# One chunk of expert weights per round, loaded as four transfers instead of one

## What is computed

```python
logits = jnp.dot(t, w_router, preferred_element_type=f32) + b_router
top_v, top_i = lax.top_k(logits, TOP_K)          # TOP_K = 4 of N_EXPERTS = 32
gates = jax.nn.softmax(top_v, axis=-1)
...
def expert_block(args):                          # xb: the tokens of expert e
    xb, e = args
    hid = xb @ w_e1[e] + b_e1[e]                 # w_e1: (32, 1024, 2048)
    gate = jnp.minimum(hid[:, :D_FF], SWIGLU_LIMIT)
    lin = jnp.clip(hid[:, D_FF:], -SWIGLU_LIMIT, SWIGLU_LIMIT)
    act = gate * jax.nn.sigmoid(SWIGLU_ALPHA * gate) * (lin + 1.0)
    return act @ w_e2[e] + b_e2[e]               # w_e2: (32, 1024, 1024)
```

## Time and profile before

| | |
|---|---|
| median of 3 runs | 1276.53 us |
| lowest and highest | 1276.32 and 1279.07 us |
| the profiled execution, its time | 1282.41 us |
| its span (first to last instruction) | 1280.3 us |
| mean granted clock of PE | 0.992 |
| PE busy | 1246.3 us (97%) |
| DVE, ACT, POOL busy | 410.8, 170.9, 113.3 us |
| DMA over the span | 455.97 MB, mean 356 GB/s |

### The profile page before, as it was taken

How to read it: one execution, slowest core, us unless ns; L and a number is a source line. 1 busy time by engine, 2 the same in 40 slices (tenths; PEclk the granted TensorE clock), 3 DMA queues, 4 the chain that set the end, 5 groups by cost and what they waited for, 6 DMA issues and landing times.

```text
span 1280.3 us, 15124 instructions
## 1 busy us (share of the span) xinstructions
PE 1246.3 (97%) x6111; PEld 561.9 (44%) x6111; DVE 410.8 (32%) x845; ACT 170.9 (13%) x299; POOL 113.3 (9%) x107
## 2 busy tenths in 40 slices
PE   8999999999999999999999999999999999999997
PEld 4488886759543333333333333333333333333332
DVE  6789685376432111211121111121111112111111
ACT  2043333011211000000100000000000000000002
POOL 4599400010000000000000000000000000000000
PEclk9999999999989999999999999999989999999999
DMA  8743476582889999999999999999999999999995
GB/s 255 174 165 132 103 149 229 204 305 82 343 312 430 425 427 426 428 427 427 429 426 428 428 426 429 429 427 429 429 425 429 427 427 430 427 427 430 428 426 244
DMA packets 56036, 455.97 MB, mean 356 GB/s; under 512 B 4888, under 2 KB 7136, under 8 KB 31024
## 3 DMA queue, kind: packets, MB, share of 16 engines
q1 hardware_dynamic: 53168, 450.80, 85.8%
q0 software_dynamic: 1664, 3.90, 2.2%
q10 hardware_dynamic: 1152, 0.52, 0.3%
HBM read 453.07 MB, written 1.61 MB: 355 GB/s over the span
## 4 chain that ended last, share of the span: by engine, by line
PE 82%; DMA 14%; ACT 2%; DVE 1%; issue 1%; SPq 0%; DVEq 0%
PE pt L1158 27%; PE pt L1181 16%; PE pt L619 10%; DMA ring<-in_w_e 10%; PE pt L646 6%; PE pt L1083 4%; PE pt L606 4%; PE pt L584 4%; PE pt L1067 3%; DMA low<-in_w_e 3%; PE pt L656 2%; PE pt L1148 2%; ACT wi_ L1328 1%; DMA stage<-in_w_in 1%; PE pt L1033 0%
## 5 line engine op out<-in xcount | busy, mean ns | idle before, releaser
L1158 PE MATMUL pt<-ring,uT_ 128*64 128x512 f32 x1192 | 266.3, 595 | 3.9 <-DMA ring<-in_w_e 3.9
L1158 PEld LDWEIGHTS pt<-ring,uT_ 128*64 128x64 f32 x1192 | 83.2, 137 | 179.1 <-issue 170.1
L2089 DVE COPY ct_<-ct_ 128x2 f32 x31 | 5.3, 170 | 452.7 <-PE pt L1158 445.3
L1181 PE MATMUL pt<-ring,wi_ 128*64 128x512 f32 x560 | 124.5, 595 | 3.7 <-ACT wi_ L1328 3.7
L1158 PE MATMUL pt<-stage,uT_ 128*64 128x512 f32 x400 | 92.6, 610 | 5.1 <-issue 3.6
L1158 PE MATMUL pt<-low,uT_ 128*64 128x512 f32 x384 | 86.3, 595 | 1.5 <-DMA low<-in_w_e 1.5
L619 PE MATMUL pt<-spare,stage 128*128 128x256 f32 x384 | 84.2, 380 | 0.0
L1511 ACT ACTIVATE wi_<-pt 128x512 f32<-128x512 f32 x32 | 19.1, 598 | 454.4 <-PE pt L1158 454.4
L2173 DVE TENSOR_SCALAR wi_<-pt 128x512 f32<-128x512 f32 x32 | 22.1, 692 | 177.7 <-PE pt L1158 177.7
L619 PEld LDWEIGHTS pt<-spare,stage 128*128 128x128 f32 x384 | 72.5, 190 | 10.6 <-issue 0.7
L1181 PEld LDWEIGHTS pt<-ring,wi_ 128*64 128x64 f32 x560 | 38.9, 137 | 77.0 <-issue 72.0
(11 more groups left out here) (354 smaller groups left out, 1267.9 us busy)
## 6 DMA issues: line engine op xcount, KB each, us to landing
ring<-in_w_e SPq DMA_DIRECT2D x112, 2048.0 KB, 27.1
low<-in_w_e SPq DMA_DIRECT2D x38, 2048.0 KB, 26.2
stage<-in_w_e SPq DMA_DIRECT2D x36, 2048.0 KB, 28.0
stage<-in_w_in SPq DMA_DIRECT2D x16, 1024.0 KB, 7.2
stage<-in_w_xkv SPq DMA_DIRECT2D x8, 1024.0 KB, 5.3
ring<-in_w_mix_out SPq DMA_DIRECT2D x4, 1024.0 KB, 9.2
stage<-in_w_xq SPq DMA_DIRECT2D x4, 1024.0 KB, 17.1
ring<-in_w_xo SPq DMA_DIRECT2D x4, 1024.0 KB, 6.8
```

The source lines that it names most:

```text
L1158: last = pe.matmul(pt[u][SLOTS * g:SLOTS * (g + 1), 512 * b:512 * (b + 1)], x[:, k % 4, k // 4], w, start=(k == 0), stop=(k == KD - 1))
L1181: last = pe.matmul(pt[u][SLOTS * h:SLOTS * (h + 1), at:at + 512], hidden[:, c, g], ring_slot[n][:, D * c + 512 * h:D * c + 512 * (h + 1)], ...
```

## The change

In rounds 1 to 5 the round's first chunk (expert 5, 10, 15, 20 or 25, chunk 0 of `w_e1`) is no longer loaded by one transfer of 128 rows but by four:

- rows 0 to 111 in full (112 rows of 16 KiB), which counts on the slot's semaphore as before;
- rows 112 to 127, columns 0 to 1023 (16 rows of 4 KiB);
- rows 112 to 119, columns 1024 to 4095 (8 rows of 12 KiB);
- rows 120 to 127, the same columns (8 rows of 12 KiB).

The last three count on `s_lead`, 48 for each round. PE waits for `s_lead` at `q * 48 + 48` as well as for the slot, ahead of that chunk. Five chunks of the 192 are touched; the bytes and their places are the same.

```diff
--- before.py
+++ after.py
@@ -40,6 +40,7 @@
 CHUNK = 4096
 HALF = CHUNK // 2
 RING = 10
+WHOLE_ROWS, SHIFTED_COLS, EIGHT = 112, 1024, 8
 W1_CHUNKS, W2_CHUNKS = 4, 2
 CHUNKS = W1_CHUNKS + W2_CHUNKS
 ROUND = 5
@@ -174,7 +175,7 @@
         s_con = sem("identity_loaded"); s_tables = sem("const_tables_loaded"); s_x = [sem(f"x_tile{t}_loaded") for t in range(NT)]; s_gain = sem("gains_loaded"); s_small = sem("s5_small_loaded")
         s_bc = sem("b_and_c_loaded"); s_par = sem("small_parameters_loaded"); s_mem = sem("mem_loaded")
         s_u4 = sem("u4_regrouped"); s_tapw = sem("taps_written"); s_tap0 = sem("lag0_taps_written"); s_toep = sem("toeplitz_loaded")
-        s_rt = sem("router_and_biases_loaded"); s_gf = sem("lower_bias_and_final_gain_loaded"); s_lead = sem("first_half_chunks_loaded")
+        s_rt = sem("router_and_biases_loaded"); s_gf = sem("lower_bias_and_final_gain_loaded"); s_lead = sem("first_half_chunks_and_shifted_rows_loaded")
         s_out = sem("out_written")
         s_slot = [sem(f"slot{i}_loaded") for i in range(STAGE)]
         s_used = sem("slots_used")
@@ -307,6 +308,15 @@
             dram, c = (w1_dram, j) if j < W1_CHUNKS else (w2_dram, j - W1_CHUNKS)
             src = dram[e, c] if isinstance(e, int) else dram[bass.ds(e, 1), c].rearrange("a p n -> p (a n)")
             eng.dma_start(ring_slot[n], src).then_inc(s_chunk[n], 16)
+
+        def load_shifted(eng, e, n):
+
+            src = w1_dram[bass.ds(e, 1), 0].rearrange("a p n -> p (a n)")
+            dst = ring_slot[n]
+            eng.dma_start(dst[0:WHOLE_ROWS], src[0:WHOLE_ROWS]).then_inc(s_chunk[n], 16)
+            eng.dma_start(dst[WHOLE_ROWS:P, 0:SHIFTED_COLS], src[WHOLE_ROWS:P, 0:SHIFTED_COLS]).then_inc(s_lead, 16)
+            for row in range(WHOLE_ROWS, P, EIGHT):
+                eng.dma_start(dst[row:row + EIGHT, SHIFTED_COLS:], src[row:row + EIGHT, SHIFTED_COLS:]).then_inc(s_lead, 16)
 
         block = ctx.enter_context(nc.Block())
 
@@ -406,16 +416,19 @@
             sp.wait_ge(S["prod"], MX + 7)
             load_page(sp, "w_xo", R21)
 
-            def load_block(e, q, r, first=0):
-
-                for j in range(first, CHUNKS):
+            def load_block(e, q, r, shifted=False):
+
+                for j in range(CHUNKS):
                     opening = isinstance(q, int) and q == 0
                     back, was = freed_by(opening, r, j)
                     if was < W1_CHUNKS:
                         sp.wait_ge(m_w1u, W1_CHUNKS * (q * ROUND + back) + was + 1)
                     else:
                         sp.wait_ge(m_w2u, W2_CHUNKS * (q * ROUND + back) + was - W1_CHUNKS + 1)
-                    load_chunk(sp, e, place_at(opening, r, j)[0], j)
+                    if shifted and j == 0:
+                        load_shifted(sp, e, place_at(opening, r, j)[0])
+                    else:
+                        load_chunk(sp, e, place_at(opening, r, j)[0], j)
 
             sp.wait_ge(S["prod"], XQ + 8)
             load_chunk(sp, 1, 8, 3)
@@ -444,7 +457,7 @@
                 load_block(r, 0, r)
             with sp.Fori(1, ROUNDS) as q:
                 for r in range(ROUND):
-                    load_block(q * ROUND + r, q, r)
+                    load_block(q * ROUND + r, q, r, shifted=(r == 0))
             for i, (b, j) in enumerate(LAST):
                 back, was = divmod(i - RING, CHUNKS)
                 if was < W1_CHUNKS:
@@ -1184,7 +1197,7 @@
                 if cs[-1] == 3:
                     last.then_inc(m_w2u, 1)
 
-            def block_of(it, q, r, early=None):
+            def block_of(it, q, r, early=None, extra=False):
 
                 pe.wait_ge(m_xT, 1 if early == 0 else it + 2)
                 for j in range(W1_CHUNKS):
@@ -1192,6 +1205,8 @@
                     pe.wait_ge(s_chunk[n], loaded)
                     if early == 0 and j == 0:
                         pe.wait_ge(s_lead, 48)
+                    elif r == 0 and j == 0 and not extra:
+                        pe.wait_ge(s_lead, q * 48 + 48)
                     if early == 0 and j == 1:
                         pe.wait_ge(m_xT, 2)
                     if j == 1:
@@ -1303,7 +1318,7 @@
                 with pe.Fori(0, EXTRA // ROUND) as g:
                     for i in range(ROUND):
                         with pe.If(n_extra > g * ROUND + i):
-                            block_of(g * ROUND + NE + i, g + (NE + i) // ROUND, (NE + i) % ROUND)
+                            block_of(g * ROUND + NE + i, g + (NE + i) // ROUND, (NE + i) % ROUND, extra=True)
             with pe.If(n_extra < 1):
                 last_blocks()
             pe.wait_ge(m_y, NE + n_extra)
```

## The result

| | before | with the change |
|---|---|---|
| median | 1278.24 us (6 runs) | 1328.62 us (6 runs) |
| lowest and highest | 1276.32 to 1279.40 us | 1322.02 to 1337.42 us |
| profiled execution, its time | 1282.41 us | 1331.54 us |
| its span | 1280.3 us | 1329.6 us |

The ratio is 1.0404, with a 95% interval of 1.0379 to 1.0429: slower by some 50 us. The forecast was 1298 us with a range of 1274 to 1316 us. The direction was right, and the size was not: 50 us instead of 22.

A forecast was written before the change was run, and what follows sets the result against it. Gapless DMA transfers were taken as the bound. Terms 4.29 + 0.59 + 4.43 = 9.31 us against 4.90 cost 4.4 us a round, 22 us in five, giving 1298 us from 1276.5, range 1274 to 1316 us.

The forecast's parts named there:

- What bounds the kernel: Expert loop: gapless DMA transfers at 428 GB/s and share 1.01 set the pace, then an untouched tail of 21.6 us.
- The ring's reserve: Rival in the expert loop: chunks already held in the ring hide the loss; given almost no chance.
- Issues and PE's wait: SP's queue and PE at a round's head: three more issues, one more wait, priced at nothing; uncovered issues 5.5 us.
- The 112 rows: Large piece of the cut chunk: runs at the full rate like 128 rows, 4.29 us a round.
- The other end: Upper bound for the 112-row piece: half the rate, 8.6 us, 4.3 us more a round.
- The 112 rows collide too: Rival: seven rows per engine break the 128-row pattern and halve the rate, 21 us more, around 1320 us; chance 0.13.
- The pieces of eight rows: Two 98.3 KB pieces of the cut chunk: 55 GB/s, 3.55 us for both, 4.43 us with another writer joining.
- a fifth writer: During the eight-row pieces, next-chunk traffic joins four writers, each getting a fifth instead of a fourth: 3.55 to 4.43 us.
- the 16 rows: The 65.5 KB piece of 4 KiB rows: 111 GB/s, 0.59 us a round, against 0.15 us at full rate.
- The main doubt of the forecast: POOL's 16-partition Toeplitz loads: their 111 GB/s might come from 512-byte pieces instead of few partitions.
- Evening out: Rival: eight-row pieces load the leading engines, so the last finishes 2.3 us sooner, 1274.2 us; chance 0.20.
- The signs: Expected in the trace: loop at about 415 GB/s, PE chunk waits before 1080 us, DMA waits about 9 + 22 us.

The follow-up runs named there:

- The twenty added transfers of eight rows: Changed kernel with whole chunks plus four unused eight-row 4 KiB transfers a round: 1289.67 us (ratio 1.0109) on neighbouring rows, 1290.30 us (1.0099) on rows four apart.
- the engines in step: Changed kernel plus SP waiting before each round until the previous chunk landed: 1320.75 us; the same wait with whole chunks: 1297.43 us.
- round 5 alone: Changed kernel with the four-transfer load only in the last of the five rounds, whole chunks in the others: 1289.84 us, ratio 1.0085.

## Why the prediction was wrong

**What bounds the kernel: right.** Nearly all of the 49 us is lost in the transfers of the loop, at an unchanged share of 1.01; nothing gives it back; the tail is still 21.7 us long. The ring's reserve hid none of it.

**Issues and PE's wait at nothing: right.** The four transfers by columns have them all, at a ratio of 0.9997.

**The 112 rows: the step that failed.** The prediction took the full rate, 4.29 us, since "112 rows lie much nearer to 128". Measured are 7.67 us each of five in a row, and 8.24 us alone. The other end that it kept, half the rate or 8.6 us, is where they are. The row that it was held nearest to was the wrong one: 128 rows are a case of their own, and 112 behave like 64. The rival "The 112 rows collide too" had this: the rate nearly halves, and with 7.67 us the term is 5 x 3.4 = 17 us more. It was given 0.13, and had neither the cheaper small pieces nor the growth, so that its 1320 us is near the measured time in part by luck. Its reason, that the engines no longer fill the partitions in the pattern of 128 rows, isn't shown by any run. The transfer needs no neighbour to be slow.

**The pieces of eight rows: mis-sized the other way.** 55 GB/s and a fifth writer made 4.43 us of two pieces. Eight neighbouring rows alone move at 91 GB/s, 1.1 us for 98.3 KB, so 2.2 us for both. In the first dip of the changed kernel their sixteen packets take 1.11 us each on the mean, and two on each of eight engines are again 2.2 us. With 0.5 us for the 16 rows (130 GB/s alone; there 0.31 us a packet) the small pieces are 2.7 us, not 5.0, which is 5 x 2.3 = 12 us less. The twenty added transfers of eight rows don't settle it: scaled to the bytes of the pieces they are 4.2 us a round by their times and 2.8 by the trace. The main doubt of the forecast, that 111 GB/s came from pieces of 512 bytes, was not what went wrong: 16 rows of 16 KiB run at 100 to 130 GB/s. The 54 GB/s for eight rows that the prediction worked out from the Trainium skill, page "SBUF — State Buffer", section "Door 1: The DMA port swizzle", don't agree with the measured 91 either.

**Sum by measured prices.** 7.7 + 0.5 + 2.2 = 10.4 us against 4.9, so 5.5 us a round. The first dip lost 5.4 us, and with the engines in step it is 4.6 us on the mean. Five times 5.5 are 27 us, close to the 22 of the forecast, because its two errors, +17 and -12 us, nearly cancel.

**The growth: missing.** The remaining 20 us (47.2 - 27) are that a late round costs more than the first, up to 12.9 us. The prediction had the engines out of step ("5.1 us behind at the end") and used it only as a gain. The runs show it the other way: the further they are out of step, the longer the packets of whole chunks on some engines run beside the cut chunk on others, and those packets are slow as well (at least 43 in round 1, 260 in round 5). Holding the engines in step took both away, and round 5 alone costs what its own spread says. Why a whole chunk's packets slow down beside the cut isn't shown. In numbers the loss of the change is 4.8 us + 0.8 x the spread to within 1 us, a fit and no more; for two halves of 64 rows it grows half as fast, from 6.7 us at a spread of 2.2 to 8.8 us at 7.4.

**Evening out: never seen.** It needed few rows at no extra cost. The dips are there in every kernel with a cut by rows, and the spread at the last dip has grown from 6.5 to 10.1 us.

**The signs.** 415 GB/s was right for the first stretch (416), too high for the others. PE's waits began before 1080 us, at 786, as forecast, and came to 49.5 us instead of 31. As a sign of collisions it named that "the 112-row transfer itself lands late". The group of those five transfers ends with

```profile
DMA to landing us min/median/max: 17.6/49.2/57.6
```

against a median of 25.2 us. Alone this would prove little, since a whole chunk into `ring` takes 34.6 us from 600 to 800 us, too, where it took 21.0: in a slower stream everything lands late. The transfers by themselves decided it.

No version beats the kernel before. Cut by columns it is the same, and every cut by rows among the kernels run is slower. Whether the engines could be evened out with transfers of every second row was not tried; the spread of 6.5 us, shared between both halves of the engines, is worth 3.3 us at most by an estimate from that spread.

## What to carry to other kernels

Cut a large load by columns and keep all 128 partitions: four pieces cost nothing here, while a cut by rows, even at 112, ran the piece at 60% of the rate and slowed the whole chunks beside it. When a stream is bound by transfers at full share, price each new shape by itself, five in a row behind the kernel's last product; a single size next to a known one ("nearly 128") is no bound. And read the first and the last occurrence of a repeated cost: here the last was 2.4 times the first.

## What was not expected of the hardware

- 112 rows of 16 KiB take 8.24 us alone and 128 rows 6.41 us; 120 rows in a row move at 203 GB/s, 48 rows alone at 123. The share of the engines says 1.00 to 1.02 at 257, 236 and 208 GB/s, so this share is no measure of bytes moved.
- For 120 rows the share is 0.94, which is 15 / 16. The Trainium skill, page "DMA: Bandwidth & Descriptors", section "Why a DMA increments its semaphore by 16 and not by 1", says that the number of engines divides the number of rows, here 15; the trace agrees, and each of these transfers has 15 counts as it lands, where the others in that kernel have 16.
- Every second row of 128 runs at 420 GB/s and 64 neighbours at 208.
- The sixteen engines of a queue drift apart: landings of one chunk are spread over 2.2 us at 463 us and 6.5 us at 1062 us in the kernel before, and nothing in that kernel brings them together again; with a wait of SP in each round it stays at 0.9 to 2.9 us. In the loop this costs nothing as long as all transfers have 128 rows.
- Whole chunks are slow beside a cut one: in round 5 at least 260 of their packets take over 700 ns instead of 614.
- One wait of SP for the chunk before it costs 4 us of stream.
